# One F32 product in place of a high and a low one, for the weighted rows of four experts in a mixture-of-experts layer

## The reference, cut to what matters

```
logits = hf @ w_router
top_val, top_idx = lax.top_k(logits, 2)
gates = softmax(top_val)
ys[expert e] = (silu(xb @ w_gate[e]) * (xb @ w_up[e])) @ w_down[e]
y[token] = sum over its two experts of gate * ys[row of the token in that expert]
h = layer_norm(ALPHA * h + y)
```

## Time and profile before

| what | value |
|---|---|
| median of 3 runs | 1894.48 us (1893.77 to 1898.86) |
| the profiled execution's own time, first to last instruction | 1894.2 us |
| TensorE busy (matmuls) | 1833.4 us, 97% of the span |
| VectorE busy | 1469.6 us, 78% |
| ScalarE busy | 1213.1 us, 64% |
| expert layer | from about 1000 us to the end |

### The profile page before, as it was taken

The page is one execution under the profiler, slowest core; times in us unless marked ns, Lnnn a source line. Parts: engine busy times, 40 slices in busy tenths (PEclk is TensorE's granted clock), DMA queues, the critical chain, the costliest instruction groups (busy, mean ns, idle before and its releaser), DMA issues.

```text
span 1894.2 us, 22429 instructions
## 1 busy us (share of the span) xinstructions
PE 1833.4 (97%) x9190; PEld 1524.4 (80%) x9190; DVE 1469.6 (78%) x1418; ACT 1213.1 (64%) x1258; POOL 142.4 (8%) x118
## 2 busy tenths in 40 slices
PE   7999999999999999999999999999999999999997
PEld 6888878888988788888788887878888787888875
DVE  5646565444579764458879899999989999998997
ACT  6555555433564454345637788988778898777784
POOL 2511100000100140004130000000000000000000
PEclk9999999999999999999989999999999999999999
DMA  8533345544442465344358999999999999999994
GB/s 296 177 134 134 134 154 204 198 178 151 170 169 89 156 224 198 134 160 154 131 202 342 373 354 423 420 422 420 395 363 362 419 420 422 418 379 368 370 420 167
DMA packets 154782, 511.54 MB, mean 270 GB/s; under 512 B 4431, under 2 KB 8898, under 8 KB 140338
## 3 DMA queue, kind: packets, MB, share of 16 engines
q1 hardware_dynamic: 152674, 504.53, 69.2%
q0 software_dynamic: 1392, 4.53, 0.7%
q10 hardware_dynamic: 608, 0.99, 0.1%
HBM read 508.98 MB, written 1.05 MB: 269 GB/s over the span
## 4 chain that ended last, share of the span: by engine, by line
PE 71%; DVE 17%; DMA 6%; ACT 3%; issue 2%; POOL 0%; ACTq 0%; SPq 0%; DVEq 0%; POOLq 0%
PE PS L442 19%; PE PS L444 19%; PE PS L443 19%; DVE WLX L1911 6%; DVE WLB L1911 6%; DMA ring<-in_moe_w_down 4%; PE PS L900 2%; PE PS L1139 1%; PE PS L1140 1%; ACT WHX L1290 1%; DMA ring<-in_moe_w_gate 1%; PE PS L1070 1%; PE PS L1072 1%; ACT WHB L1290 1%; PE PS L596 1%
## 5 line engine op out<-in xcount | busy, mean ns | idle before, releaser
L1911 DVE TENSOR_TENSOR WLB<-ring,WHB 128x2048 fp32r<-128x2048 f32 (+1 forms) x344 | 636.6, 1867 | 113.2 <-ACT WHB L1290 112.7
L1290 ACT ACTIVATE WHB<-ring 128x2048 fp32r<-128x2048 f32 (+1 forms) x344 | 531.5, 1557 | 300.1 <-PE PS L444 270.6
L1911 DVE TENSOR_TENSOR WLX<-ring,WHX 128x2048 fp32r<-128x2048 f32 (+1 forms) x216 | 469.1, 2192 | 51.2 <-ACT WHX L1290 51.0
L1290 ACT ACTIVATE WHX<-ring 128x2048 fp32r<-128x2048 f32 (+1 forms) x216 | 392.6, 1834 | 156.4 <-PE PS L444 124.8
L442 PE MATMUL PS<-WHB,XH 128*128 128x512 f32 (+1 forms) x640 | 255.2, 399 | 8.6 <-DVE XL L1945 2.4
L444 PE MATMUL PS<-WHB,XL 128*128 128x512 f32 (+1 forms) x640 | 247.7, 387 | 0.0
L443 PE MATMUL PS<-WLB,XH 128*128 128x512 f32 (+1 forms) x640 | 247.1, 386 | 0.0
L442 PEld LDWEIGHTS PS<-WHB,XH 128*128 128x128 f32 x640 | 121.1, 189 | 36.7 <-issue 6.2
L2831 POOL TENSOR_TENSOR SM<-SM,MH 128x8 f32<-128x8 f32 (+3 forms) x28 | 38.1, 1366 | 1392.1 <-DVE SM L1924 1392.1
L444 PEld LDWEIGHTS PS<-WHB,XL 128*128 128x128 f32 x640 | 120.8, 189 | 25.0
L443 PEld LDWEIGHTS PS<-WLB,XH 128*128 128x128 f32 x640 | 121.3, 190 | 21.8
(11 more groups left out here) (422 smaller groups left out, 3407.6 us busy)
## 6 DMA issues: line engine op xcount, KB each, us to landing
ring<-in_moe_w_gate SPq DMA_DIRECT2D x56, 2048.0 KB, 11.1
ring<-in_moe_w_up SPq DMA_DIRECT2D x56, 2048.0 KB, 10.9
ring<-in_moe_w_down SPq DMA_DIRECT2D x56, 2048.0 KB, 11.7
ring<-in_w_in SPq DMA_DIRECT2D x13, 2048.0 KB, 7.8
ring<-in_hg_w_in SPq DMA_DIRECT2D x8, 2048.0 KB, 8.4
ring<-in_da_w_in SPq DMA_DIRECT2D x6, 2048.0 KB, 7.9
ring<-in_w_gate SPq DMA_DIRECT2D x5, 2048.0 KB, 7.5
ring<-in_w_up SPq DMA_DIRECT2D x5, 2048.0 KB, 7.6
```

The lines of the kernel that those rows point to most:

```text
L1290: e.activation(hi, src, ACT.Copy).then_inc(s_hi, 1)
L1911: e.tensor_tensor(lo, src, hi.bitcast(F32), ALU.subtract).then_inc(s_lo, 1)
```

## The change

Four of the light experts, 1, 2, 4 and 5, are PLAIN. For them ScalarE writes the weighted rows whole, as F32, into ZF (which shares its place with ZH); VectorE writes no low part; and TensorE makes one F32 product of POT, read as F32, and ZF in place of two products in FR. For these experts ScalarE itself signals s_zl, and VectorE's count of s_zh leaves them out. The other four experts are as before.

```diff
+PLAIN = (1, 2, 4, 5)
...
+            with ExitStack() as part2:
+                ZF = part2.enter_context(nc.sbuf_tensor("ZF", [128, D], F32))
             ZH = pt("ZH", [128, D], FR)
...
-                e.matmul(PS[b][:, :], POT[:, tt, :], ZH[:, cs], start=True, stop=False)
-                e.matmul(PS[b][:, :], POT[:, tt, :], ZL[:, cs], start=False, stop=True).then_inc(banks.put(("cb", ex, k), b, out=(s_add, 4 * ex + k + 1)), 1)
+                if ex in PLAIN:
+                    t = e.matmul(PS[b][:, :], POT[:, tt, :].bitcast(F32), ZF[:, cs], start=True, stop=True)
+                else:
+                    e.matmul(PS[b][:, :], POT[:, tt, :], ZH[:, cs], start=True, stop=False)
+                    t = e.matmul(PS[b][:, :], POT[:, tt, :], ZL[:, cs], start=False, stop=True)
+                t.then_inc(banks.put(("cb", ex, k), b, out=(s_add, 4 * ex + k + 1)), 1)
...
-                    e.activation(ZH[:, 512 * q:512 * q + 512], PS[4 + q], ACT.Copy, scale=GS[ex]).then_inc(s_zh, 1)
+                    if ex in PLAIN:
+                        e.activation(ZF[:, 512 * q:512 * q + 512], PS[4 + q], ACT.Copy, scale=GS[ex]).then_inc(s_zl, 1)
+                    else:
+                        e.activation(ZH[:, 512 * q:512 * q + 512], PS[4 + q], ACT.Copy, scale=GS[ex]).then_inc(s_zh, 1)
...
             def down_out(ex):
+                if ex in PLAIN:
+                    return
                 v.wait_ge(s_pot, 2 * ex + 2)
+                n = 2 * (ex - sum(x < ex for x in PLAIN))
                 for q in range(2):
-                    v.wait_ge(s_zh, 2 * ex + q + 1)
+                    v.wait_ge(s_zh, n + q + 1)
```

## The result

| | before | after |
|---|---|---|
| median of 20 runs | 1894.48 us (1892.37 to 1898.86) | 1897.93 us (1895.77 to 1900.04) |
| span of the profiled execution | 1894.2 us | 1895.7 us |

The ratio is 1.0017, with a 95% interval of 1.0011 to 1.0024: 3.2 us more, between 2.1 and 4.5 (3.45 between the two medians). The forecast was 1897.7. The kernel's own time, which the median is taken from, is some 1.8 us longer than the span of its trace.

What follows compares the result with a forecast made beforehand. Transfers were taken to bound light experts, TensorE heavy ones. Heavy +3.2 us, light TensorE, VectorE and the rest 0, on a span of 1894.2 plus 0.3 to the median: 1897.7 us, range 1892.5 to 1901.0.

Steps and rivals of the forecast that it cites:

- TensorE in heavy experts: Eight changed products in heavy experts 3 and 6, where TensorE has no gap: 0.40 us more each, +3.2 us.
- Rival (e): The F32 product is not run as L1165's is: at 1.18 us the eight cost 5.8 us, 1900.3; chance 0.03.
- TensorE in light experts: Eight changed products in light experts 2 and 5: 3.2 us more work, covered by TensorE's gaps, costed at nothing.
- rival (d): TensorE decides in light experts 2 and 5 too: all sixteen products cost 6.5 us, 1901.0; chance 0.10.
- VectorE: Four pairs of low parts, 1.41 us each, go in experts 2, 3, 5 and 6: 5.6 us less work, worth nothing.
- Rival (c): VectorE sets the pace in light experts: two pairs return 2.8 us, less 3.2, so 1894.9; chance 0.13.
- rival (b): TensorE's extra cost is hidden in heavy experts too: the 3.2 us falls away, 1894.5; chance 0.12.
- The new lateness: Products end about 0.4 us later before VectorE's add (L2664); tightest room 1.1 us, 0.7 after: no cost.
- The sum: Whole kernel: +3.2 us on the 1894.2 us span gives 1897.4; the median, 0.3 above the span, makes it 1897.7.

Runs made afterwards that it cites:

- the two halves of PLAIN: PLAIN cut to experts 1 and 4, or to 2 and 5, against the kernel before: 1893.93 us, ratio 1.0000, and 1897.95 us, ratio 1.0015.
- the first four experiments: PLAIN (1, 4); PLAIN (2, 5); VectorE's low part dropped; extra F32 products in light experts; against the kernel before: ratios 1.0000, 1.0015, 1.0001, 1.0003.
- the last version: PLAIN set to experts 0, 1, 3, 4 and 6, against the kernel before: 1892.36 us, ratio 0.9985.

## Why the prediction was right

**TensorE in heavy experts: +3.2 forecast, 3.6 measured.** The place and the mechanism hold, shown by the two halves of PLAIN. The size was 0.40 a product and is 0.45. The term compared the chain's spacing of L1165 (0.86) with 0.46; the matmul behind the combine is at once 0.42 later, and the whole interval gives 0.45. Most of the difference is in the matmuls behind the product: TensorE is 0.42 later at the second and 0.45 from the eighth on, and a whole product takes 0.91 and not 0.86. The chain's 1.72 us for two products of L1165 leaves out what the matmuls behind them lose. Why those follow wider isn't shown. Rival (e), 1.18 us a product, falls.

**TensorE in light experts: 0 forecast, 0 measured,** and rival (d) falls: even one more F32 product for each combine costs nothing there. I had seen 3.7 and 2.9 us of gaps; the cover is at least the 3.6 us of four whole products.

**VectorE: 0 forecast, 0 measured.** Rival (c) falls for this change; the landing times fit a slot freed sooner that only queues longer. But my picture of the margin was wrong. I read from a median landing time of 12.1 us that more than one load's time always lies ahead, so that VectorE should have room; 2.8 us more on VectorE in each of two places cost 5.6 in all by the medians. The median says nothing of the thinnest moment of the queue, and VectorE's 91.14 of 93 us was the warning.

**Hidden in heavy experts, rival (b),** falls: the intervals grow by the full 1.8 us. With it falls, for this kernel, the measure by the busy share of weight loads (the Trainium skill, "Perfetto Trace Analysis", "Identifying the Most-Contended Engine"): at 109.11 of 130 us, 84%, TensorE had no room at all. With 128x512 products back to back a matmul starts 0.23 us after the last, and a weight load takes 188 ns, so a TensorE without any room shows some 82%, not 100.

**The new lateness: no cost, as forecast.** The add that I had found to have least room starts at 1374.13 in the changed kernel, with no idle ahead of it:

```profile
1371.92 2.29 DVE L1921 TENSOR_TENSOR WLX<-ring,WHX 128x2048 fp32r<-128x2048 f32 x1 [0.39 <-ACT WHX L1297]
1374.13 0.68 DVE L2677 TENSOR_TENSOR H<-H,PS 128x512 f32<-128x512 f32 x1
```

**The sum.** One step was wrong and did no harm, by luck: the profiled execution's own time is not its span. The one of after took 1897.45 us with a span of 1895.7, 1.75 more. By that, the one of before took about 1895.9 (an estimate), some 1.5 above its median; it holds the half-clock stretch of the earlier trace rows, 1.6 us, which the one of after doesn't have. So the two spans differ by 1.5 where the medians differ by 3.45. The forecast came out because the 0.3 us that it added brought it to the median plus 3.2.

## What to carry to other kernels

Before trading one engine's work for another's, find for each place of the trade which engine or queue is without a gap there, and put the dearer product only where its engine has gaps: here the combines of five experts fall in such places and those of two don't, and choosing those five turned +3.2 us into -2.8 (with VectorE's relief moved to where it is late). Relief of an engine that is nearly tied with another gave nothing here, or about a microsecond where that engine was late, while more work for it cost in full by the medians; so a test that takes work away and one that adds work must both be run before a slack is believed.

## What I had not expected of the hardware

The spread of the runs goes in good part with TensorE's clock. Among the 33 runs of the kernel before beside the first four experiments the fastest, 1890.53 us, had a mean granted clock of 0.994, and the slowest, 1899.06, one of 0.989; over all 33 the correlation of time and mean clock is -0.65. A half-clock stretch came after a gap of 1.23 us on TensorE, where the program goes from a light to a heavy expert, and two more after the gaps of 2.90 and 2.91 us behind VectorE's extra work. But the length of the last gap alone doesn't decide: before 1194.36 us the changed kernel has one of 1.76 us and keeps its clock, and before 1192.91 us the last version has one of 0.49 and loses it. At the place of the earlier trace rows the profiled execution of after stays at the upper level (1.00 for 1628 to 1770 us, above, against 0.99).
